# Expert weights in 19 lasting slots and one used once, refills by halves, gather and scatter moved between the columns

## The reference

```python
for e in range(N_EXPERTS):            # 32 experts
    act = jax.nn.silu(hf @ w_g[e]) * (hf @ w_u[e])
    y = y + combine[:, e:e + 1] * (act @ w_d[e])   # two experts per token have a weight
x = x + gate2 * y
```

## Time and profile before

| what | value |
|---|---|
| median of 3 runs | 1379.45 us (1378.80 to 1379.68) |
| profiled execution, own time | 1379.51 us |
| its span | 1377.7 us |
| TensorE busy | 1329.3 us (96%) |
| DMA queue of SP | 355.49 MB, 65.5% of 16 engines' span |
| experts on TensorE, first to last column | 233.15 to 676.45 us |

### The profile page before, as it was taken

The page is one execution under the profiler, slowest core; times in us unless marked ns, Lnnn a source line. Parts: engine busy times, 40 slices in busy tenths (PEclk is TensorE's granted clock), DMA queues, the critical chain, the costliest instruction groups (busy, mean ns, idle before and its releaser), DMA issues.

```text
span 1377.7 us, 21079 instructions
## 1 busy us (share of the span) xinstructions
PE 1329.3 (96%) x8758; PEld 1003.9 (73%) x8758; DVE 634.7 (46%) x1423; ACT 298.0 (22%) x595; POOL 9.0 (1%) x20
## 2 busy tenths in 40 slices
PE   8999999999999988888999999999999999999997
PEld 5888886453343334333588789999998878999996
DVE  2477465121001000010378847775455784777454
ACT  2234102112111111111243521220013352122000
POOL 0000000000000000000000000000000000000000
PEclk9999999999999999999999999999999999999999
DMA  9997787899999999999954144445444414454510
GB/s 392 363 414 269 302 355 258 330 421 420 421 421 421 421 421 421 421 421 421 420 224 154 62 153 153 172 165 173 164 155 153 153 62 153 154 183 156 182 62 32
DMA packets 52545, 365.15 MB, mean 265 GB/s; under 512 B 6225, under 2 KB 6529, under 8 KB 9441
## 3 DMA queue, kind: packets, MB, share of 16 engines
q1 hardware_dynamic: 49680, 355.49, 65.5%
q10 hardware_dynamic: 1888, 5.04, 1.3%
q0 software_dynamic: 880, 3.24, 0.6%
HBM read 359.28 MB, written 2.37 MB: 263 GB/s over the span
## 4 chain that ended last, share of the span: by engine, by line
PE 83%; DMA 14%; DVE 1%; ACT 1%; issue 0%; DVEq 0%; SPq 0%
PE bank L1224 26%; PE bank L647 20%; PE bank L962 15%; DMA ring<-in_weights 10%; PE bank L659 5%; DMA ringx<-in_weights 4%; PE bank L975 2%; PE bank L1369 2%; PE bank L1160 2%; PE bank L775 2%; PE bank L947 1%; PE bank L1273 1%; PE bank L1324 1%; PE bank L719 1%; PE bank L1350 1%; PE bank L1337 1%
## 5 line engine op out<-in xcount | busy, mean ns | idle before, releaser
L962 PE MATMUL bank<-ring,cst 128*64 128x512 f32 x632 | 174.6, 594 | 13.9 <-DMA ring<-in_weights 9.8
L647 PE MATMUL bank<-h,ring 128*128 128x256 f32 x832 | 184.1, 381 | 0.1
L647 PEld LDWEIGHTS bank<-h,ring 128*128 128x128 f32 x832 | 157.2, 190 | 22.4 <-issue 1.7
L962 PEld LDWEIGHTS bank<-ring,cst 128*64 128x64 f32 x632 | 55.8, 137 | 104.1 <-issue 104.1
L1224 PE MATMUL bank<-hid,ring 128*128 128x128 f32 x912 | 115.6, 276 | 0.0
L1224 PE MATMUL bank<-h,ring 128*128 128x128 f32 x896 | 113.8, 276 | 0.0
L2144 DVE TENSOR_TENSOR act<-act,bank 128x512 f32<-128x512 f32 x16 | 11.0, 688 | 220.8 <-PE bank L962 220.8
L1224 PEld LDWEIGHTS bank<-hid,ring 128*128 128x128 f32 x912 | 108.6, 192 | 0.0
L962 PE MATMUL bank<-ringx,cst 128*64 128x512 f32 x272 | 100.6, 594 | 7.0 <-DMA ring<-in_weights 5.7
L1224 PEld LDWEIGHTS bank<-h,ring 128*128 128x128 f32 x896 | 107.0, 192 | 0.1
L962 PE MATMUL bank<-ring,a_s 128*64 128x512 f32 x328 | 92.4, 596 | 3.2 <-ACT a_s L1529 3.2
(11 more groups left out here) (397 smaller groups left out, 1846.6 us busy)
## 6 DMA issues: line engine op xcount, KB each, us to landing
ring<-in_weights SPq DMA_DIRECT2D x264, 1024.0 KB, 12.1
ringx<-in_weights SPq DMA_DIRECT2D x49, 1024.0 KB, 26.0
pool_a<-in_weights SPq DMA_DIRECT2D x9, 1024.0 KB, 26.1
x<-in_weights SPq DMA_DIRECT2D x9, 1024.0 KB, 26.0
x<-in_x SPq DMA_DIRECT2D x1, 1024.0 KB, 5.1
pool_a<-in_cst ACTq DMA_DIRECT2D x1, 1024.0 KB, 6.3
bias<-bias_rows POOLq DMA_DIRECT2D x1, 1024.0 KB, 17.0
x_all<-in_weights SPq DMA_DIRECT2D x1, 1024.0 KB, 6.7
```

The source lines that it names most:

```text
L647: ins = e.matmul(u.ap[:, 0:S], w[:, k * width + j * P:k * width + (j + 1) * P], acts[:, k, :], start=k == 0, stop=k == kc - 1)
L962: ins = e.matmul(g.bank[bank][ex * SLOTS:(ex + 1) * SLOTS, :], stat(m, ex), block, start=first and m == 0, stop=last and m == blocks - 1)
```

## The change

The two slots of pieces, `BESIDE` and `SPREAD`, are given up, and with them the trip of `rope` to DRAM and back. 20 tiles are loaded early instead of 22. `AHEAD` stays the one slot used once and holds tile 19; 19 slots are refilled in turn, now from tile 20 on, so that tile n lies where tile n - 20 (n below 39) or n - 19 (from 39 on) was. Tiles 20 to 37 (`BY_HALVES`) are refilled by halves of 512 KB, and every pair of tiles raises `half_used`. `x_t` is written to DRAM just before its own slot is filled, which is now the first use of `KEPT`. On TensorE half 0 of the scatter goes between gate and up columns, half 1 stays behind the up columns in every pair (the last pair had its own order), and the gather goes between the two down columns.

```diff
@@ -142,10 +142,11 @@
 RL = 8
 UPS = 14
 SEVENS = UPS + 15
-AHEAD, BESIDE, SPREAD, KEPT = range(R + RX, R + RX + 4)
-FIRST_SLOTS = (R + 5, R + 3, R + 2, 0, 1, 2, 3, 4, 5, AHEAD, R, R + 1, 6, 7, 8, 9, 10, R + 4, 11, BESIDE, SPREAD, KEPT)
-ONCE = {3: SPREAD, 6: AHEAD, 7: BESIDE}
+AHEAD, KEPT = R + RX, R + RX + 1
+FIRST_SLOTS = (R + 5, R + 3, R + 2, 0, 1, 2, 3, 4, 5, AHEAD, R, R + 1, 6, 7, 8, 9, 10, R + 4, 11, KEPT)
+ONCE = {19: AHEAD}
 EARLY = len(FIRST_SLOTS)
+BY_HALVES = range(EARLY, 38)
 
 
 def first_slots():
@@ -170,7 +171,7 @@
 
 def pieces(t):
 
-    return {3: 4, 7: 2, EARLY: 2, EARLY + 1: 2}.get(t - T_EXP, 1)
+    return 2 if t - T_EXP in BY_HALVES else 1
 
 
 def slots():
@@ -192,7 +193,7 @@
         "cact_ready cact_spread ada_rows ada_turned ada_placed select_ready squares sq_added recip root h_scaled h_shifted trig_ready rope_ready lb_diff lb_exp "
         "dve_step shift_routed rms_ready route_exp_in route_exp_out picked summed x_placed starts_ready most_known x_moe xw x_out "
         "row_max row_exp prob mixed1 "
-        "mix_half o_half col_a col_b half_used x_kept rope_kept pick_ready pickw_ready gathered x_dve gy_act gy_dve "
+        "mix_half o_half col_a col_b half_used x_kept pick_ready pickw_ready gathered x_dve gy_act gy_dve "
         "silu_done act_ready act_turned a_copied put_turned put_ready last_scattered "
         "over_ready over_filled over_diag over_cb over_cbs over_gate over_up over_silu over_mul over_a over_done over_h "
         "sig_ready forget log_in log_f keys cum_ready "
@@ -226,8 +227,7 @@
         self.nc, self.dram, self.out = nc, dram, out
         sem = lambda n: ctx.enter_context(nc.semaphore(n))
         self.s = {n: sem(n) for n in SEMS}
-        self.slot_filled = [sem(f"slot_filled_{i}") for i in range(R + RX + 4) if i != BESIDE]
-        self.slot_filled.insert(BESIDE, self.slot_filled[AHEAD])
+        self.slot_filled = [sem(f"slot_filled_{i}") for i in range(R + RX + 2)]
         self.bank_full = [sem(f"bank_full_{i}") for i in range(8)]
         self.bank_free = [sem(f"bank_free_{i}") for i in range(8)]
         self.step = Count(self.s["dve_step"])
@@ -308,8 +308,7 @@
 
     def filled(self, e, t):
 
-        both = [o + T_EXP for o in ONCE if ONCE[o] in (AHEAD, BESIDE)]
-        e.wait_ge(self.slot_filled[SLOT[t]], 16 * (sum(map(pieces, both)) if t in both else USE[t] + pieces(t)))
+        e.wait_ge(self.slot_filled[SLOT[t]], 16 * (USE[t] + pieces(t)))
         return self.ring[SLOT[t]]
 
     def hand_back(self, ins):
@@ -412,8 +411,7 @@
     g.top = gate_off
     g.gy = g.area("gy", D)
     g.ring += [g.area(f"ringx{n}", TILE) for n in range(RX - 1)] + [g.pool_a]
-    g.ring += [x_all[:, 2 * KC * P:4 * KC * P], (x_all[:, KC * P:2 * KC * P], g.gy[:, :]),
-               (g.act[:, :], g.a_s[:, :], g.rope[:, :], g.p("pool_w")), g.x_t]
+    g.ring += [x_all[:, 2 * KC * P:4 * KC * P], g.x_t]
     assert KC * P == D == TILE // 2
     g.x_s = g.c("lnmask", 0, KC * P).rearrange("p (k t) -> p k t", k=KC)
     assert g.top <= mod_off
@@ -527,11 +525,6 @@
             g.full(sp, "pol", 3)
         elif SLOT[t] == R + 4:
             sp.wait_ge(g.s["ada_placed"], 12)
-        elif SLOT[t] == BESIDE:
-            g.full(sp, "h_tok", 3)
-        elif SLOT[t] == SPREAD:
-            g.full(sp, "h_tok", 3)
-            sp.wait_ge(g.s["rope_kept"], 16)
         elif SLOT[t] == KEPT:
             sp.wait_ge(g.s["x_kept"], 16)
             sp.wait_ge(g.s["squares"], SQUARES[1] + KC)
@@ -553,25 +546,22 @@
     w = g.dram["weights"]
     sp.dma_start(g.x_t[:, :], g.dram["x"]).then_inc(g.s["x_in"], 16)
     for t in [*range(T_EXP), *(T_EXP + n for n in FIRST_TILES)]:
-        if SLOT[t] == BESIDE:
+        if SLOT[t] == KEPT:
             sp.wait_ge(g.s["h_scaled"], 2 * KC)
             sp.dma_start(g.dram["x_kept"], g.x_t[:, :]).then_inc(g.s["x_kept"], 16)
         slot_free(sp, g, t)
-        if pieces(t) == 1:
-            sp.dma_start(g.ring[SLOT[t]][:, :], w[t]).then_inc(g.slot_filled[SLOT[t]], 16)
-        else:
-            width = TILE // pieces(t)
-            for h in range(pieces(t)):
-                sp.dma_start(g.ring[SLOT[t]][h], w[t][:, h * width:(h + 1) * width]).then_inc(g.slot_filled[SLOT[t]], 16)
-    for h in range(2):
-        for ex in range(2):
-            t = T_EXP + EARLY + ex
-            if h:
-                slot_free(sp, g, t)
-            else:
-                sp.wait_ge(g.s["half_used"], 2)
-            sp.dma_start(g.ring[SLOT[t]][:, h * D:(h + 1) * D], w[t][:, h * D:(h + 1) * D]).then_inc(g.slot_filled[SLOT[t]], 16)
-    for t in range(T_EXP + EARLY + 2, T_LAYERS):
+        sp.dma_start(g.ring[SLOT[t]][:, :], w[t]).then_inc(g.slot_filled[SLOT[t]], 16)
+    for n in BY_HALVES[::2]:
+        for h in range(2):
+            for ex in range(2):
+                t = T_EXP + n + ex
+                if h:
+                    slot_free(sp, g, t)
+                else:
+                    sp.wait_ge(g.s["half_used"], 2 * ((BEFORE[t] - T_EXP) // 2 + 1))
+                part = slice(h * D, (h + 1) * D)
+                sp.dma_start(g.ring[SLOT[t]][:, part], w[t][:, part]).then_inc(g.slot_filled[SLOT[t]], 16)
+    for t in range(T_EXP + BY_HALVES[-1] + 1, T_LAYERS):
         slot_free(sp, g, t)
         sp.dma_start(g.ring[SLOT[t]][:, :], w[t]).then_inc(g.slot_filled[SLOT[t]], 16)
     n = max(t for t in range(T_EXP, T_LAYERS) if SLOT[t] == KEPT) - T_EXP
@@ -956,12 +946,9 @@
     pair = [g.filled(e, tile + ex) for ex in range(2)]
     for m in range(blocks):
         for ex in range(2):
-            w = pair[ex]
-            per = blocks // len(w) if isinstance(w, tuple) else 0
-            block = w[m // per][:, m % per * 512:(m % per + 1) * 512] if per else w[:, m * 512:(m + 1) * 512]
-            ins = e.matmul(g.bank[bank][ex * SLOTS:(ex + 1) * SLOTS, :], stat(m, ex), block,
-                           start=first and m == 0, stop=last and m == blocks - 1)
-            if m == 1 and tile == T_EXP:
+            ins = e.matmul(g.bank[bank][ex * SLOTS:(ex + 1) * SLOTS, :], stat(m, ex),
+                           pair[ex][:, m * 512:(m + 1) * 512], start=first and m == 0, stop=last and m == blocks - 1)
+            if m == 1:
                 ins.then_inc(g.s["half_used"], 1)
             if m == blocks - 1:
                 ins.then_inc(g.s["col_b" if ex else "col_a"], 1)
@@ -991,7 +978,6 @@
         g.idle(e, n)
     for p in range(PAIRS):
         tile, b = T_EXP + 12 * p, 2 * (p % 2)
-        last = p == PAIRS - 1
         x = lambda half: lambda m, ex: g.x_s[:, 4 * half + m, ex * SLOTS:(ex + 1) * SLOTS]
         a = lambda m, ex: g.a_s[:, m * P + ex * SLOTS:m * P + (ex + 1) * SLOTS]
         if p:
@@ -1000,27 +986,25 @@
             if p == 0:
                 e.wait_ge(s["x_placed"], 2 * half + 2)
             pe_columns(e, g, tile + 2 * half, b, 4, x(half), half == 0, half == 1)
+        if p:
+            pe_scatter(e, g, p - 1, 0)
         for half in range(2):
             pe_columns(e, g, tile + 4 + 2 * half, b + 1, 4, x(half), half == 0, half == 1)
         if p:
-            pe_scatter(e, g, p - 1, 0)
-            if not last:
-                pe_scatter(e, g, p - 1, 1)
+            pe_scatter(e, g, p - 1, 1)
         e.wait_ge(s["act_ready"], p + 1)
         for f in range(EC):
             ins = e.transpose(g.bank[b][:, f * P:(f + 1) * P], g.act[:, f * P:(f + 1) * P], g.c("ident"))
         ins.then_inc(s["act_turned"], 1)
-        if last:
-            pe_scatter(e, g, p - 1, 1)
         e.wait_ge(s["pickw_ready"], p + 1)
         for tt in range(ST):
             ins = e.transpose(g.bank[b + 1][:, tt * P:(tt + 1) * P], g.pickw[:, tt * P:(tt + 1) * P], g.c("ident"))
         ins.then_inc(s["put_turned"], 1)
+        e.wait_ge(s["a_copied"], p + 1)
+        pe_columns(e, g, tile + 8, b, EC, a, True, True)
         if p < CHUNKS - 1:
             e.wait_ge(s["pick_ready"], p + 2)
             pe_gather(e, g, 2 - b)
-        e.wait_ge(s["a_copied"], p + 1)
-        pe_columns(e, g, tile + 8, b, EC, a, True, True)
         e.wait_ge(s["put_ready"], p + 1)
         pe_columns(e, g, tile + 10, b + 1, EC, a, True, True)
     for half in range(2):
@@ -2271,7 +2255,6 @@
     e.tensor_tensor(g.D[1], g.D[0], g.D[1], ALU.add).then_inc(s["at_sum"], 1)
 
     cos, sin = (g.rope[:, o:o + S].unsqueeze(1).to_broadcast([P, 2, S]) for o in (0, S))
-    e.wait_ge(s["rope_kept"], 32)
     for i in range(4):
         c = 2 * (i % 2)
         s2, r2 = (g.cq if i < 2 else g.ck)[:, c:c + 2, :], (g.cq_turned if i < 2 else g.ck_turned)[:, c:c + 2, :]
@@ -2576,14 +2559,11 @@
         o = 0 if qt == 0 else HEADS * P
         e.dma_start(g.bias[:, o:o + HEADS * nk].rearrange("p (h k) -> p h k", h=HEADS), src).then_inc(s["bias_in"], 16)
     e.wait_ge(s["bias_in"], 32)
-    e.wait_ge(s["rope_ready"], 2)
-    e.dma_start(g.dram["rope"], g.rope[:, :]).then_inc(s["rope_kept"], 16)
     g.full(e, "pol", 3)
```

(2 more changed lines are left out.)

## The result

| | before | after |
|---|---|---|
| median of 6 runs each | 1379.57 us (1378.80 to 1380.01) | 1384.15 us (1382.21 to 1386.06) |
| ratio, 95% interval | | 1.0035 [1.0023, 1.0047] |
| profiled execution: own time, span | 1379.51, 1377.7 us | 1383.99, 1382.2 us |
| L, landing of tile 187 | 661.34 | 661.67 |
| D, end of the last columns | 676.45 | 675.57 |

The changed kernel is 0.35% slower, 4.5 us in the span. `h` stands 4.49 us later, which is the whole of it: up to D the change wins 0.9 us, and between D and `h` it loses 5.4.

What follows compares the result with a forecast made beforehand. The prediction took full DMA engines, landing expert weights, to bound the late pairs, with the layer waiting behind the last columns. 1379.51 - 2.2 - 1.3 + 6.8 gave 1382.8 us, range 1379.7 to 1385.6.

Steps and rivals of the forecast that it cites:

- Refills: Expert stage's start: closing the refill gap lands tile 41, then tile 187, earlier by 2.2 us.
- Gather: Between the two down columns: moving it there costs nothing beyond the refill term, 0.
- Last pair: From L to D: half the scatter ahead of the up columns shortens the chain from 15.11 to 13.84 us, -1.3.
- What stands behind the last tile: From D to `h`: residual reload and layer weights wait for the last matmul, and TensorE's clock falls, +6.8 us.
- Rivals 1, 3 and 4: Clock stays up, 1380.2, chance 0.13; reload hidden, 1376.0 to 1378.3, 0.07; more before the first layer tile, 1385, 0.10.
- Rival 1: Behind the last scatter: TensorE's idle time ends before its clock is taken down; 1380.2 us, chance 0.13.
- rival 2: At tile 41: the queue never dries as down columns end by 287.4, -4.1 instead of -2.2; 1380.9 us, chance 0.10.
- rival 5: Stage's start: 18 tiles by halves move at 360 GB/s, 7.6 us more; end at 1388.5, chance 0.05.

Runs made afterwards that it cites:

- e4: e1 with the gather ahead of both down columns again, as in the kernel before; 1378.78 us, ratio 0.9995.
- e1: Changed kernel with tiles 190 and 191 in the slots of tiles 172 and 173, so the last tile in `x_t` is 171; 1378.55 us, ratio 0.9994.
- e7: Kernel before, with only the last pair's scatter split as in the changed kernel; 1378.41 us, ratio 0.9991.
- e2: Kernel before, but SP reloads the residual only when tile 190's last matmul has ended; 1385.58 us, ratio 1.0046.
- e3: Changed kernel plus four matmuls that nothing reads behind the last scatter; 1382.25 us, ratio 1.0021.
- e8: e6 with tiles 20 and 21 whole too, so no refill by halves at all; 1377.72 us, ratio 0.9987.
- e6: e1 with the changes of e4 and e5 together; 1377.52 us, ratio 0.9991 as recorded.
- e9: The same kernel as e6, run again with more rounds; 1378.05 us, ratio 0.9988.
- e5: e1 with only tiles 20 and 21 refilled by halves, all others whole; 1378.07 us, ratio 0.9990.
- e10: e1 plus 200 extra waits on GpSimd in each of the 16 pairs, 3200 instructions; 1382.03 us.

## Why the prediction was right, and where not

The time forecast was 1382.8 us and 1384.15 was measured, within the range of 1379.7 to 1385.6, and the direction was right. By its terms:

| step | forecast | measured |
|---|---|---|
| Refills (L) | -2.2 | +0.3 |
| Gather | 0 | not separable from 0 (e4 against e1: +0.2) |
| Last pair (L to D) | -1.3 | -1.2 |
| What stands behind the last tile (D to `h`) | +6.8 | +5.4 |
| sum | +3.3 | +4.5 |

**Last pair: right.** 13.90 us instead of 13.84, and e7 shows the gain by itself.

**What stands behind the last tile: the mechanism right, the size 1.4 too large.** e1 and e2 show it from both sides. In order: the reload was issued at D, as forecast; VectorE's add began at D + 4.9 and not D + 5.4; TensorE's first layer tile at D + 7.4 and not D + 8.2, because an empty queue delivered the reload in 4.8 us where I had taken the 5.4 of the earlier trace rows, and the tile followed 2.5 us behind it with nothing from GpSimd's constants in front. The clock cost 1.95 us (8.86 against 6.91; by e3 and e1, whose first tiles take 7.17 and 7.22 at the full clock, 0.3 of it isn't the clock) and not the 2.6 of the earlier trace rows. 0.8 and 0.65 are the 1.4. My upper bound of 3.5 for "a whole first tile at the low level" was worked out wrongly: a whole tile at half the clock takes another 6.9 us, by an estimate from the 6.91 at the full one. The clock came back before the tile's end in both runs. I had also put VectorE and TensorE level at +4.2; VectorE's last sum before the matmul of sums (L624 at 691.82) ends at 690.06, so TensorE was the one waited for. Rivals 1, 3 and 4 fall: the clock did go down, the reload was not hidden, the tile landed earlier than forecast and not later. Rival 1 was nearer than its 0.13 says: TensorE stood for 3.7 us and not 4.5, and the clock still read 1.00 up to 683, the moment at which the tile began.

**Refills: the step that failed.** Its term, -2.2, was measured at +0.3. I wrote that tiles 20 to 40 "would be in at" 290.3, or a microsecond later, and that tile 41, issued at 289.3, would find the queue dry and land at 294.7. The issue was right (289.8). But tile 40 landed at 293.3, so nothing was dry, and tile 41 came one tile's time behind it. That is what rival 2 has in its name, but not its reason or its gain: the queue held because the tiles ahead were late. The missing 3 us are in two rates. For 12 us from 236 the engines moved 348 GB/s and not 421, which is 12 x 73 / 421 = 2.1 us; I had allowed one, for 3 us of the slow rate. For 30 us more they moved 410, 0.8 us. With these the sum is 290.3 + 2.9 = 293.2, and tile 41 one tile's time later. Both rates come with the halves, as far as e8's one execution shows it (420 GB/s from the start, 422 later). The error lies in how I read the earlier trace rows: I took the 360 GB/s of 239 to 242 for a queue with too little in it, "since its second part was whole tiles". But of the 293 packets of that stretch 292 are under 8 KB, so all of it was halves (tiles 22 and 23, which land at 242.6 and 244.2). From the DMA view of that stretch before:

```profile
DMA packets 293, 1.08 MB, mean 360 GB/s; under 512 B 30, under 2 KB 30, under 8 KB 292
```

The gain at tile 41 was 1.0 us, and at tile 53 still 1.0 (325.6 against 326.7), in this pair of executions: e1, with the very same start, has tile 41 at 297.5, later than before.

Then it was lost on the way to tile 187: the changed kernel's trace has two long steps there (343.0 to 347.2 and 573.3 to 577.2), that of before one (478.4 to 482.4), each 1.4 to 1.7 us over 2.49. The account closes: from tile 41 to 187 are 146 steps of 2.486 us, 363.0, and with the excess of the long ones before gives 296.9 + 363.0 + 1.5 = 661.4 (661.34 measured), the changed kernel 295.8 + 363.0 + 1.7 + 1.4 = 661.9 (661.67), e1 with one long step 297.5 + 363.0 + 1.5 = 662.0 (661.74). Each long step has its instruction packet, and which packets make one differs between executions of one kernel; e6 and e9, one kernel, differ by 1.8 us in L. So closing the gap was done as described, and in the changed kernel and e1 what it gained by the end lies within what executions of one kernel differ by. With whole tiles a part does seem to arrive. By the medians e5, e6, e9 and e8 are 1.3, 1.9, 1.5 and 1.9 us below the kernel before, where the split scatter alone (e7) is 1.0 below it. That would be 0.3 to 0.9 us for the refills, of the 2.2 forecast; the recorded intervals don't separate it from nothing.

By the list in the prediction, L above 662 would have spoken for rival 5 (halves slow): L was 661.67, yet halves are slow, only not for long at 360 GB/s. Their price in the changed kernel is that of the two rates, about 2.9 us up to tile 40, not 7.6, and the earlier first issue gives 2.4 of it back.

**The sum** was 1.2 us short because the first term was 2.5 too hopeful and the last 1.4 too dear. It came close partly because two errors of opposite sign met; the sign of the result rested on the last term, and that held.

**A version that beats both.** With the tile in `x_t` an early one, the last pair's split scatter, 20 early tiles and no halves (e8), the kernel takes 1377.72 us (1377.38 to 1378.03), 0.9987 [0.9978, 0.9996] of before: 1.9 us, in all of its 11 runs below all 21 of before. It is also the simplest of them, without `BESIDE`, `SPREAD` and refills by halves.

## What to carry to other kernels

When slots are renumbered, look at which buffer holds the last items of a stage and who must have it back first: an in-order queue that waits for that buffer hides everything behind it, here a whole layer's weights, and a single index (e1) decided 5.6 us. Price such an exposed wait as transfer, plus the next transfer, plus TensorE's low clock, and check whether cheap unread work can hold the clock (e3: 1.9 us). And ask of a gain in a stage full of transfers whether it is larger than what one execution differs from the next there; here 1 us in a single trace was not. When a stretch is slow, look at the sizes of its packets before you call it a queue with too little in it.

## What the runs showed of the hardware that I had not expected

- Instruction packets share the DMA engines with the weights. One of 16 KB takes 1.06 us on one engine, and when all are full some of them push every later landing back by 0.5 to 1.7 us for good. Ten more of GpSimd's 8 KB packets in the expert stage cost 3.4 us (e10 against e1), from 3200 waits of which nearly all had nothing to wait for.
- A stream of refills that begins with transfers of 512 KB moves 358 to 392 GB/s in 239 to 251 us (the changed kernel, e1, e3 to e6 and e9); the one that begins with whole tiles of 1 MB (e8) moves 420 there. After that it is 410 (halves) or 422 (whole tiles, e5 and e8).
- A transfer of 1 MB issued into an empty queue landed 4.8 to 4.9 us later behind the experts (the reload, in the changed kernel, e2 and e3) and at their start in e8 (its first refill), and 5.4 us later in the gap of the kernel before.
